# Attention scores of the prompt in three rounded products, and the output weights loaded late

## The reference, cut to what matters

```python
def stick_breaking_attention(q, k, v, bias, q_offset):
    scale = q.shape[-1] ** -0.5                     # head dimension 64, 16 heads
    for start in range(0, tq, Q_BLOCK):             # blocks of 128 queries
        ...
        z = jnp.einsum('bqhd,bkhd->bhqk', qb, kb) * scale + bias_f
        causal = s_pos[None, :] < t_pos[:, None]
        log_one_minus = jnp.where(causal, jax.nn.log_sigmoid(-z), 0.0)
        after = lax.cumsum(log_one_minus, axis=3, reverse=True) - log_one_minus
        w = jnp.where(causal, jnp.exp(jax.nn.log_sigmoid(z) + after), 0.0)
        o = jnp.einsum('bhqk,bkhd->bqhd', w, vb)
    return jnp.concatenate(outs, axis=1)
...
m = o.reshape(b, t, N_HEADS * HEAD_DIM) @ p['w_o'][j]
```

## Time and profile before

| | |
|---|---|
| median of 3 runs | 3095.6 us (3095.36 to 3097.46) |
| the profiled execution | 3093.14 us, its span 3091.2 us |
| PE busy | 3053.9 us, 99% |
| DVE busy | 1967.8 us, 64% |
| ACT busy | 1374.9 us, 44% |
| POOL busy | 211.5 us, 7% |
| the chain that ended last | PE 87%, DVE 8%, ACT 2%, issue 2%, DMA 1% |
| the attention, first page turned to last product | about 1462 to 2205 us |

### The profile page before, as it was taken

The page is one execution under the profiler, slowest core; times in us unless marked ns, Lnnn a source line. Parts: engine busy times, 40 slices in busy tenths (PEclk is TensorE's granted clock), DMA queues, the critical chain, the costliest instruction groups (busy, mean ns, idle before and its releaser), DMA issues.

```text
span 3091.2 us, 59913 instructions
## 1 busy us (share of the span) xinstructions
PE 3053.9 (99%) x23618; PEld 2591.5 (84%) x23618; DVE 1967.8 (64%) x2953; ACT 1374.9 (44%) x2349; POOL 211.5 (7%) x391
## 2 busy tenths in 40 slices
PE   8999999999999999999999999999999999999998
PEld 7987888888999998998666666666788888899998
DVE  6998677644655345533877877877567763565522
ACT  5445633233333333323767777777543233333322
POOL 0212000000000002221111110011000000000000
PEclk9999999999999999999999999999999999999999
DMA  4222233333333335647999999999623333333232
GB/s 130 80 77 82 82 89 95 96 106 113 107 93 89 96 104 182 193 145 226 358 390 383 382 382 385 389 394 371 231 86 92 96 94 111 110 110 89 84 109 86
DMA packets 482233, 534.47 MB, mean 173 GB/s; under 512 B 22129, under 2 KB 400362, under 8 KB 481752
## 3 DMA queue, kind: packets, MB, share of 16 engines
q1 hardware_dynamic: 467254, 482.90, 46.3%
q0 software_dynamic: 14608, 47.55, 4.6%
q10 hardware_dynamic: 92, 0.19, 0.0%
HBM read 486.84 MB, written 33.89 MB: 168 GB/s over the span
## 4 chain that ended last, share of the span: by engine, by line
PE 87%; DVE 8%; ACT 2%; issue 2%; DMA 1%; SPq 0%; DVEq 0%; POOL 0%; ACTq 0%; POOLq 0%
PE PS L1132 59%; PE PS L2223 8%; PE PS L2259 4%; PE PS L2236 4%; DVE mT L935 4%; PE PS L2274 3%; PE PS L2284 2%; PE PS L2293 2%; DVE wlo L363 1%; PE PS L2245 1%; PE PS L652 1%; ACT whi L358 1%; PE PS L1774 1%; PE PS L696 0%; PE PS L1005 0%
## 5 line engine op out<-in xcount | busy, mean ns | idle before, releaser
L363 DVE TENSOR_TENSOR wlo<-raw,whi 128x1024 fp32r<-128x1024 f32 (+1 forms) x368 | 442.0, 1201 | 572.4 <-ACT whi L358 559.4
L358 ACT CAST whi<-raw 128x1024 fp32r<-128x1024 f32 (+1 forms) x368 | 379.3, 1031 | 951.7 <-PE PS L1132 911.5
L1132 PE MATMUL PS<-xfh,whi 128*128 128x512 f32 (+2 forms) x2240 | 621.5, 328 | 0.8 <-DVE wlo L363 0.5
L1132 PE MATMUL PS<-xfh,wlo 128*128 128x512 f32 (+2 forms) x2240 | 618.9, 327 | 0.0
L1132 PE MATMUL PS<-xfl,whi 128*128 128x512 f32 (+2 forms) x2240 | 617.9, 327 | 0.0
L1132 PEld LDWEIGHTS PS<-xfh,whi 128*128 128x128 f32 x2240 | 378.9, 188 | 40.7 <-issue 3.6
L1132 PEld LDWEIGHTS PS<-xfl,whi 128*128 128x128 f32 x2240 | 379.3, 188 | 36.8 <-issue 0.5
L1132 PEld LDWEIGHTS PS<-xfh,wlo 128*128 128x128 f32 x2240 | 378.4, 188 | 36.3
L1132 PE MATMUL PS<-pA,whi 128*128 128x272 f32 (+1 forms) x1536 | 332.5, 324 | 0.0
L2223 PE MATMUL PS<-ident,kr 128*128 128x128 f32 x2048 | 276.7, 276 | 0.5 <-ACT kt L2380 0.5
L2223 PEld LDWEIGHTS PS<-ident,kr 128*128 128x128 f32 x2048 | 225.9, 140 | 46.8 <-issue 45.9
(11 more groups left out here) (355 smaller groups left out, 4926.2 us busy)
## 6 DMA issues: line engine op xcount, KB each, us to landing
kr<-in_cache_k SPq DMA_DIRECT2D x256, 512.0 KB, 6.5
vr<-in_cache_v SPq DMA_DIRECT2D x256, 512.0 KB, 6.3
raw<-in_ffn_w_gate SPq DMA_DIRECT2D x88, 512.0 KB, 3.7
raw<-in_ffn_w_up SPq DMA_DIRECT2D x88, 512.0 KB, 3.7
raw<-in_ffn_w_down SPq DMA_DIRECT2D x64, 512.0 KB, 3.9
raw<-in_ffn_w_down SPq DMA_DIRECT2D x32, 384.0 KB, 3.3
raw<-in_conv_w_glu SPq DMA_DIRECT2D x16, 512.0 KB, 4.1
raw<-in_conv_w_out SPq DMA_DIRECT2D x16, 512.0 KB, 4.0
```

Of the source, the lines that this page charges most:

```text
L358: nc.scalar.copy(whi[b][:, 0:blocks_of(t), :], raw[t % RAWS][:, 0:blocks_of(t), :]).then_inc(w_hi, 1)
L363: nc.vector.tensor_tensor(wlo[t % RAWS][:, 0:n, :], raw[t % RAWS][:, 0:n, :], whi[b][:, 0:n, :].bitcast(F32), ALU.subtract).then_inc(w_lo, 1)
L1132: mm = nc.tensor.matmul(PS[:, s + c, 0:c1 - c0], stationary(wt, t, kw + k), x(k0 + k)[:, c0:c1], start=start and k == 0 and wt is whi and ...
```

## The change

The prompt's scores are made as the weight products are. Of each pair's keys and queries ACT makes a high part (`k_high`, `q_high`, 128 x 1024 each) and DVE a low part, written over `kp` and `qp` (`k_low`, `q_low`). A unit's scores are then three products per head in `float32r` in place of one in float32. The high parts lie where `raw` 0 and 1 and `whi` 0 and 1 were, so the first two tiles of `w_o` can't wait there any more: they are loaded and split near the attention's end (tile 0 loaded at page 240, split at the end of phase 125; tile 1 loaded once all scores are made, split at the end of phase 131). The waits `w_o_split` are gone. The first pair is split before phase 0, the later ones in the pair before theirs, the keys at the end of the phase that is the pair's eighth, the queries at the end of its twelfth (`PAIR_AT`).

```diff
-        X_OUT, X_FFN, X_KV, X_Q = (1, 9), (3, 11), 5, 7
+        X_OUT, X_FFN, X_KV, X_Q, X_PAIR = (1, 11), (3, 13), 5, 7, 9
...
         def next_hi(act, t):
-            if t + 2 < TILES:
+            if t + 2 < TILES and t + 2 not in (first["out10"], first["out10"] + 1):
                 split_hi(act, t + 2, t // RING + 1, t % RING)
...
                 if x % 32 == 12 and x // 32 + 1 < PAIRS:
                     load_pair(x // 32 + 1)
+                if x == NPG - 16:
+                    sp.wait_ge(a_pv, PER_PAIR * (PAIRS - 1))
+                    load_w_o(sp, 0)
+                if x == NPG + 3:
+                    sp.wait_ge(a_z, NU)
+                    load_w_o(sp, 1)
...
                 if i == 0:
                     pe.wait_ge(a_ld[pr % 2], 48 * (pr // 2 + 1))
+                    pe.wait_ge(n_lo, KB * X_PAIR + 2 * pr + 2)
                 if u >= 1:
                     pe.wait_ge(a_sg, 4 * u)
-                for hh in range(2):
-                    r = slice(HD * hh, HD * hh + HD)
-                    mm = nc.tensor.matmul(PS[:, 4 + hh, 0:w], qp[pr % 2][r, i * P:(i + 1) * P],
-                                          kp[pr % 2][r, 512 * kc:512 * kc + w], start=True, stop=True)
+                for q, k in ((qh, kh), (qh, kl), (ql, kh)):
+                    for hh in range(2):
+                        r = slice(HD * hh, HD * hh + HD)
+                        mm = nc.tensor.matmul(PS[:, 4 + hh, 0:w], q[pr % 2][r, i * P:(i + 1) * P],
+                                              k[pr % 2][r, 512 * kc:512 * kc + w], start=k is kh and q is qh, stop=q is ql)
                 mm.then_inc(a_z, 1)
...
+        PAIR_AT = {16 * pr - 16 + p: (pr, j) for pr in range(1, PAIRS) for j, p in enumerate((7, 11))}
+
+        def pair_high(act, pr, j):
+            b = pr % 2
+            act.wait_ge(a_ld[b], 48 * (pr // 2 + 1))
+            if pr >= 2:
+                act.wait_ge(a_pv, PER_PAIR * (pr - 1))
+            nc.scalar.copy((kh, qh)[j][b][:], (kp, qp)[j][b][:]).then_inc(n_hi, 1)
+
+        def pair_low(dve, pr, j):
+            b = pr % 2
+            dve.wait_ge(n_hi, KB * X_PAIR + 2 * pr + j + 1)
+            nc.vector.tensor_tensor((kl, ql)[j][b][:], (kp, qp)[j][b][:], (kh, qh)[j][b][:].bitcast(F32), ALU.subtract).then_inc(n_lo, 1)
...
             q_done(act)
-            w_o_split(act)
             tok_all_stored(act)
+            for j in range(2):
+                pair_high(act, 0, j)
...
                 if chunk_scored(p) is not None:
                     page_rests(chunk_scored(p))
+                if p in PAIR_AT:
+                    pair_high(act, *PAIR_AT[p])
                 for k in ATT_BLOCKS.get(p, ()):
                     attention_high(act, k)
+                if p == PHASES - 7:
+                    split_hi(act, w_o_tile(0), 0, w_o_tile(0) % RING)
+                if p == PHASES - 1:
+                    split_hi(act, w_o_tile(1), 0, w_o_tile(1) % RING)
...
                 if unit_scored(p) is not None:
                     prompt_remainders(unit_scored(p))
+                if p in PAIR_AT:
+                    pair_low(dve, *PAIR_AT[p])
...
+                if p == PHASES - 7:
+                    split_lo(dve, w_o_tile(0), w_o_tile(0) % RING)
+                if p == PHASES - 1:
+                    split_lo(dve, w_o_tile(1), w_o_tile(1) % RING)
...
-            for n in range(2):
-                t = first["out10"] + n
-                load_tile(sp, t, t % RING, cols(A["w_o"][0], n), KB)
             mix_sp(sp)
```

More of the change, by code:

```diff
@@ L145, in yoco_step @@
     RW, RSW, QSW = 1032, 1032, DB * PAIRS * 32
-    spot = [AR_AT]
+    spot, where = [AR_AT], {}
     def stack(name, shape, dt=F32):
@@ L151, in stack @@
             n *= s
+        where[name] = spot[0]
         t = at(name, shape, dt, spot[0])
@@ L198, in yoco_step @@
     sq = [at(f"sq{k}", [P, T], F32, AR_AT + (8 + k) * ROW) for k in range(KB)]
+    kl, ql = ([at(f"{n}_low{b}", [P, NP], F32R, where[f"{n}p{b}"]) for b in range(2)] for n in "kq")
+    kh = [at(f"k_high{b}", [P, NP], F32R, WT_AT + 4096 * b) for b in range(2)]
+    qh = [at(f"q_high{b}", [P, NP], F32R, WT_AT + 4096 * (RAWS + b)) for b in range(2)]
     raw = [at(f"raw{j}", [P, KB, P], F32, WT_AT + j * 4096) for j in range(RAWS)]
@@ L1393, in out_dve0 @@
             if layer == 1:
-                dve.sem_inc(n_t, 2 * KB)
+                dve.sem_inc(n_t, 4 * KB)
         BLOCKS_IN = ((), (0,), (1, 2), (3, 4), (5,), (6, 7), (), ())
@@ L2041, in q_done, with w_o_tile, load_w_o @@
             eng.wait_ge(w_used, first["out10"] + 2)
-        def w_o_split(eng):
-            eng.wait_ge(w_lo, first["out10"] + 4)
+        def w_o_tile(n):
+            return first["out10"] + n
+        def load_w_o(sp, n):
+            load_tile(sp, w_o_tile(n), w_o_tile(n) % RING, cols(A["w_o"][0], n), KB)
         def set_read(eng, s):
@@ L2194, in mix_sp @@
             q_done(sp)
-            w_o_split(sp)
             for x in range(V_EARLY, VR):
@@ L2533, in mix_dve @@
             tok_all_stored(dve)
-            w_o_split(dve)
             nc.vector.memset(ws[:], 0.0).then_inc(a_one, 1)
@@ L2540, in mix_dve @@
             dve.wait_ge(s_z, 1)
+            for j in range(2):
+                pair_low(dve, 0, j)
             for p in range(PHASES):
@@ L2791, in _ @@
             q_done(pool)
-            w_o_split(pool)
             att_pool(pool)
```

## The result

| | median us | lowest to highest | runs |
|---|---|---|---|
| before | 3096.8 | 3093.6 to 3099.8 | 9 |
| after | 3105.4 | 3100.7 to 3109.0 | 9 |

The ratio is 1.003, with a 95% interval of 1.0021 to 1.0038: slower by a little more than this kernel's runs can tell from no change. The forecast was 3098.5. In the two profiled executions the time went from 3093.1 to 3106.1 us and the span from 3091.2 to 3104.1, 12.9 more, against 2.9 forecast.

A forecast was written before the change was run, and what follows sets the result against it. PE was taken to set the pace, with transfers keeping up. Scores -11.8, pairs' splits +12.7, start +1.0 and end +1.0 gave +2.9: 3093.1 to 3096.0 us profiled, 3098.5 as median; range 3085 to 3108.

The forecast's parts named there:

- the forecast's own range: The whole kernel's time if the forecast of 3098.5 us holds: 3092 to 3105 us, given 40%.
- The splits' cost: Seven pairs, eighth and twelfth phases: late key copies delay PE's transposes 0.77 and 1.05 us, 12.7 us in all.
- The rival of hidden splits: Pairs' and tile 0's splits fit into DVE's idle time, so 12.7 and 1.0 us go: 3085 us, 20%.
- The units: Prompt's scores as three rounded products: 0.87, 0.70, 0.53, 0.50 us for 512, 384, 256, 128 keys; 11.8 us saved.
- float32's price for narrow products: Scores with 128 keys: narrow rounded products cost four cycles a column, 5.9 us more, 3104 us, 18%.
- loads in the open: Prompt's scores: weight loads don't overlap the running product, 0.21 us a unit, 20 us more, 3119 us, 6%.
- heads in turn: Prompt's scores: two heads' products run one after the other, six steps for three, 52 us more, 3151 us, 6%.
- PE sets the pace: Attention's middle: PE waited 1.4 us in 457, never for a transfer; a us off its chain is one off the time.
- The sign that I had named for being right: A middle pair's sixteen phases get longer by 0.3 us: less 1.5 from scores, plus 1.8 from splits.
- The delay spreads: After the twelfth phase DVE stays late through two more, PE waits 0.5 us an insertion: 7 us, 3105 us, 10%.
- The start: Before the first scores: w_o's split goes, two subtractions of 1.14 us precede the first key copies; 1.0 us longer.
- the end: Tile 0's split in phase 125 delays the key copy and the transposes after it: 1.0 us longer.

## Why the prediction was right and where it failed

The time lies inside the range and the direction is the side that had the largest chance, by little, but it is 6.9 us above the forecast and just over the forecast's own range. Step by step:

*The splits' cost* was right in place, chain and size: 0.77 and 1.05 us forecast for the two places, 0.89 and 1.06 measured with the splits alone. That the order on ACT, not the load of DVE, makes the cost is shown by moving the cast: it goes to nothing. The sentence that PE was never waiting there, so that nothing absorbs the delay, holds for these two places. The rival of hidden splits did not come true, by the order on ACT that the prediction held against it; with the cast moved, it does.

*The units* were nearly right: 0.87, 0.70, 0.53 and 0.50 forecast, 0.89, 0.73, 0.55 and 0.48 measured. The term was mis-sized by 0.19 us a pair, 1.5 in all: the first step is 0.33 us where I had 0.23 and a share of the switching. Of the rivals, float32's price for narrow products would have made 0.87 of the unit with 128 keys, loads in the open 1.08 of the one with 512, and heads in turn 1.56. All three are refuted by the units' rows.

Of the loads the Trainium skill ("TensorE: Matmul & The Clock Gate", Part 3, What overlaps and what doesn't) says that they overlap a running matmul only where the row groups differ. The load at 1905.81 goes to the rows on which the product of 1905.71 runs, and the unit takes 0.89 us, so the trace does not agree.

*"PE sets the pace", on the strength of 1.4 us of waits*, and so a us off the scores being a us off the time: this is the step that failed. PE waited some 1.2 us in every pair, in the fourth, eighth and twelfth phases, for DVE's key copies; the wait hid behind matmul ends that are modelled, and showed only as a part of the 32.3 us of idle weight loads, 7.5 us of them by the run that takes it away. A gain on PE ahead of such a place is absorbed by it. That took 0.51 us of each pair, 4.1 in all, 40% of the gain; with the copies made earlier the whole 1.29 us comes through in four of the six middle pairs, and 1.17 in the other two. The sign that I had named for being right, a middle pair longer by 0.3 us, came out as 1.18: 0.51 of it is this step, 0.19 the units and 0.13 the splits. The condition that I had written beside the rule, that a us off the scores is a us off the time "as long as PE doesn't come to wait for something else", was not tested phase by phase.

*The delay spreads* (3105) named nearly the time that came, and its mechanism is refuted: fourteen phases of the kernel with the splits alone are unchanged. A time that fits doesn't show a cause. Its sign, "phases thirteen to fifteen longer than before", was badly put: by the forecast itself the thirteenth had to be longer, by 1.05 less what its unit gains. It is, by 0.90; the fourteenth and fifteenth are 0.17 shorter.

*The start* came to 0.75 for 1.0, and *the end* to 1.1 for 1.0. The end's chain in the kernel after is as written, cast, subtraction, key copy, transposes:

```profile
2191.40 1.04 ACT whi L362
...
2193.61 0.70 DVE kt L2497
...
2194.44 0.63 PE PS L2298 x4
2195.07 0.89 PE PS L2288 x6
```

That tile 1 and the extra loads on SP's queue cost the attention nothing is borne out by the kernel with the late tiles alone, whose other phases are unchanged. Behind the attention PE waits once for the low part of a later `w_o` tile, 1.9 us before and 2.5 after (PE's waits from 2236 to 2248, and of the kernel after from 2248 to 2260):

```profile
PE PS L1132 <- DVE wlo L363: 1.9, 1, 1.9
```

```profile
PE PS L1136 <- DVE wlo L367: 2.5, 1, 2.5
```

The tile's load took 10.3 us to land before, 10.8 after, 11.9 with the late tiles alone, and 11.0 in the kernel where only DVE's order had changed. It varies without the change too, so the half us isn't shown to be the change's; the last 400 us of the kernel are shorter by 0.6 us, and the remainder of 0.5 in the table stays open.

*What I had no term for* is TensorE's clock. The same stretch ahead of the attention, before and then after (the columns of the earlier trace rows; the last three numbers are the granted clock, the DMA share and GB/s):

```profile
1425.00:1430.00 5.00, 3.92 (x17) 3.25 (x18) 1.84 (x2) 1.72 (x3) 0.70 (x2) 1.00 1.09 361
```

```profile
1425.00:1430.00 5.00, 3.76 (x10) 3.02 (x11) 1.52 (x2) 1.84 (x3) 0.56 (x1) 0.66 1.08 361
2254.00:2259.00 5.00, 4.56 (x13) 3.64 (x14) 2.72 (x4) 1.93 (x4) 0.00 (x0) 0.66 0.22 66
```

In the profile of the kernel after, the granted clock over each of two stretches of 5 us was 0.66 on average: within them it was at its lower level, 1.2 GHz, for a while. The first shows 10 products where before shows 17. What stands behind each place comes 1.5 to 1.6 us later (a third of 5 us, 1.7, is what the clock withheld). What both places share is a PE that had just stood idle, waiting for the low part of a weight tile: 2.1 us until 1426.24, and the 2.5 us shown above, until 2254.44. The kernel before waits at the same two places, 2.1 and 1.9 us, and its profiled execution had neither drop, so the idle time alone doesn't decide, and why one execution has a drop and another hasn't stays open. The 12.9 us between the profiles hold 3.1 that I put down to no edit; the medians differ by 8.6.

## What to carry to other kernels

Before you count a saving on the busiest engine in full, look phase by phase for waits that the saving would run into; where an engine's ends are modelled, read the idle time of its weight loads, and compare how long the same two neighbours lie apart in different phases. When work is added to a helper engine, its place behind what it waits for counts for more than its length: here the same cast and subtraction cost 1.95 us a pair behind the sigmoid and nothing ahead of it. Moving the splits took 15 us off the changed kernel, moving one running product 13.5 off the kernel before, and the change itself, with both in place, is worth 5.6.

## What the hardware showed that I had not expected

- Rounded products on half of the rows: two heads' products start 3 ns apart, and three such steps take 0.89 us at 512 columns and 0.48 at 128. Going from 512 to 128 columns saves less than half.
- The clock's drops come and go between executions. The seven other kernels of this study had them near 1425 or 1427, 1467 or 1469, 2210, 2233, 2240 or 2246 us, three kernels two and four one. All ten, and the two of the kernel after, lie within about 1 us of the end of a wait of PE of 1.8 to 3.5 us, for a weight tile's low part or, near 1467, for the first pair's `q_low` (2.4 us, a wait that the change brought in); twelve such waits of 1.8 to 2.6 us had no drop. In one with early splits, where PE had waited 2.2 us until 2239.26:

```profile
2239.00:2244.00 5.00, 4.74 (x14) 3.77 (x15) 2.54 (x4) 1.75 (x3) 0.00 (x0) 0.66 0.28 85
```

Two runs of the kernel after with a mean granted clock of 0.998 took 3100.7 us, seven with 0.995 or 0.996 took 3104.7 to 3109.0. At 1.5 us each the drops explain a part of that only. They make some of the spread of 6 to 8 us between executions of one kernel, which is why single runs were read here by the lengths of their phases. These are equal from pair to pair within 0.02 us in the middle pairs of every kernel but the two fastest.
